# The last product of a gated merge block, eight token tiles in pairs by Strassen's scheme

## The reference, cut to what matters

```python
yb = ob @ w_o_dsa[l]                       # [1024, 1024] @ [1024, 1024]
ga, gb = jnp.split(jax.nn.sigmoid(gl), 2, axis=-1)
out = (ga * ya + gb * yb) @ w_out[l]       # the last product
x = x + gate[:, None] * out
return rms_norm(x, final_g)
```

## Time and profile before

| what | us |
|---|---|
| median of 3 runs (1383.16 to 1385.47) | 1385.27 |
| the profiled execution's own time | 1384.56 |
| its span, first to last instruction | 1382.8 |
| granted TensorE clock, mean over the span | 0.995 |
| busy: PE, DVE, ACT, POOL | 1340.8, 934.3, 705.9, 590.5 |

### The profile page before, as it was taken

The page is one execution under the profiler, slowest core; times in us unless marked ns, Lnnn a source line. Parts: engine busy times, 40 slices in busy tenths (PEclk is TensorE's granted clock), DMA queues, the critical chain, the costliest instruction groups (busy, mean ns, idle before and its releaser), DMA issues.

```text
span 1382.8 us, 26267 instructions
## 1 busy us (share of the span) xinstructions
PE 1340.8 (97%) x10010; PEld 808.4 (58%) x10010; DVE 934.3 (68%) x1894; ACT 705.9 (51%) x1461; POOL 590.5 (43%) x653
## 2 busy tenths in 40 slices
PE   6899999999999999999999999999999999899997
PEld 6456994444444556666666666655445777644444
DVE  4889877777334577678778776545834999737444
ACT  4767777785432654565665654333123777501111
POOL 0084677778762433632623521003021788665000
PEclk9999999999999999999999999999999999999999
DMA  9401333333324231322322322335675888975222
GB/s 367 149 8 32 109 111 105 115 123 107 115 87 131 70 88 49 92 64 64 92 64 63 93 64 77 107 107 211 201 237 184 148 157 161 153 270 178 74 92 92
DMA packets 213416, 166.36 MB, mean 120 GB/s; under 512 B 92482, under 2 KB 185514, under 8 KB 211628
## 3 DMA queue, kind: packets, MB, share of 16 engines
q1 hardware_dynamic: 212444, 160.20, 40.7%
q10 hardware_dynamic: 720, 4.46, 0.8%
q0 software_dynamic: 128, 0.03, 0.0%
HBM read 114.40 MB, written 31.15 MB: 105 GB/s over the span
## 4 chain that ended last, share of the span: by engine, by line
PE 50%; DVE 7%; issue 4%; POOL 3%; DMA 2%; ACT 1%; SPq 0%; DVEq 0%; ACTq 0%; POOLq 0%
PE ps L94 13%; PE ps L95 13%; PE ps L96 13%; DVE g_yq L1655 1%; DVE g_o L2581 1%; POOL g_shared L1420 1%; POOL g_shared L1422 1%; PE ps L1938 1%; PE ps L2062 1%; PE ps L2046 1%; PE ps L2045 1%; PE ps L2041 1%; PE ps L2061 1%; PE ps L1976 1%; DVE g_piece_hi L2592 1%
## 5 line engine op out<-in xcount | busy, mean ns | idle before, releaser
L94 PE MATMUL ps<-g_h_hi,g_piece_hi 128*128 128x512 f16 x544 | 206.9, 380 | 1.6 <-PEq L2689 1.6
L96 PE MATMUL ps<-g_h_hi,g_piece_lo 128*128 128x512 f16 x544 | 206.5, 380 | 0.0
L95 PE MATMUL ps<-g_h_lo,g_piece_hi 128*128 128x512 f16 x544 | 206.5, 380 | 0.0
L1420 POOL TENSOR_TENSOR g_shared<-g_shared 128x120 f32<-128x120 f32 (+14 forms) x120 | 56.3, 469 | 180.3 <-DMA g_shared<-diagonal_blocks 170.0
L1042 DVE TENSOR_SCALAR_CACHE_REDUCE a_ada<-a_ada,a_s_all 128x896 bf16<-128x896 f32 (+1 forms) x124 | 112.9, 967 | 1.0
L94 PE MATMUL ps<-g_o,g_h_hi 128*128 128x128 f16 (+2 forms) x424 | 102.0, 269 | 10.2 <-DMA g_o<-g_piece 7.6
L1655 DVE SCALAR_TENSOR_TENSOR g_yq<-e_raw,g_taps,g_yq 128x1024 f32<-128x1024 f32 x60 | 91.1, 1518 | 22.5 <-ACT g_yq L1484 20.7
L95 PE MATMUL ps<-g_o,g_h_hi 128*128 128x128 f16 (+2 forms) x424 | 101.8, 269 | 0.0
L96 PE MATMUL ps<-g_o,g_h_lo 128*128 128x128 f16 (+2 forms) x424 | 101.8, 269 | 0.0
L96 PEld LDWEIGHTS ps<-g_h_hi,g_piece_lo 128*128 128x128 bf16 x544 | 53.2, 98 | 64.3
L94 PEld LDWEIGHTS ps<-g_h_hi,g_piece_hi 128*128 128x128 f16 x544 | 53.2, 98 | 53.4 <-issue 2.0
(11 more groups left out here) (438 smaller groups left out, 4000.6 us busy)
## 6 DMA issues: line engine op xcount, KB each, us to landing
a_w<-in_w_in SPq DMA_DIRECT2D x17, 1024.0 KB, 5.8
g_piece<-in_w_in SPq DMA_DIRECT2D x34, 512.0 KB, 4.2
channel_gates<-a_ada SPq DMA_DIRECT2D x48, 256.0 KB, 2.2
g_shared<-diagonal_blocks SPq DMA_DIRECT2D x32, 256.0 KB
a_ada<-in_w_ada ACTq DMA_DIRECT2D x4, 1024.0 KB, 9.6
a_x<-in_x SPq DMA_DIRECT2D x8, 512.0 KB, 9.0
delta_gate<-a_ada SPq DMA_DIRECT2D x16, 256.0 KB, 2.6
g_shared<-sums_by_head SPq DMA_DIRECT2D x8, 512.0 KB, 4.1
```

The lines of the kernel that those rows point to most:

```text
L94: pe.matmul(out, a_hi, b_hi, start=first, stop=False)
L95: pe.matmul(out, a_hi, b_lo, start=False, stop=False)
L96: return pe.matmul(out, a_lo, b_hi, start=False, stop=last)
L1420: nc.gpsimd.tensor_tensor(part, table[:, j, :, j + 1:BASE], tc[:, :, j:j + 1].broadcast_to([P, NT, left]), ALU.mult).then_inc(sub, 1)
```

## The change

The last product is done for pairs of token tiles, tile i with tile i+4, in four groups. A group is a 2x2 block product: rows are the two tiles, the inner dimension is two halves of 512, and columns are two halves of 512. It is done in seven block products of 12 matmuls each, which add up in three PSUM banks: x takes products 0, 2, 4 and 6, y takes 1, z takes 3 and 5. Between them ScalarE copies a bank's state out (`keep`), since some results are partial sums. Each quarter of `w_out` (128 + 128 of its columns) now yields seven 128x512 operands, not four, and so does each group of tokens: three plain blocks and four sums or differences. GpSimd forms these four, all in place but the tokens' first. The merged half is no longer cast as it comes; it is kept in float32 (`m32`), scaled by SHRINK.

Who does what: ScalarE casts all seven `hi`; GpSimd makes the `lo` of the three plain blocks and the four sums; VectorE makes the `lo` of the four sums. `o` items stay as they were on GpSimd. SP loads a `w_out` item, and an `o` item, in two DMAs of 128 columns.

```diff
@@ SP @@
+                for half in range(2):
+                    c0 = u * UNIT + half * P if which == "o" else u * P + half * BANK
+                    sp.dma_start(w32[:, j % 2, :, half * P:(half + 1) * P], (wo if which == "o" else wv)[:, :, c0:c0 + P]).then_inc(w_in[j % 2], 16)
...
             for n in range(16):
+                sp.dma_start(m32[b // 4][:, b % 4, cols], g.m_dram[b * P:(b + 1) * P, cols]).then_inc(m_in[n % 4], 16)
                 if n >= 4:
                     sp.wait_ge(summed, n - 3)
+                sp.dma_start(gb[:, n % 4], g.sig_dram[2 * D + b * P:2 * D + (b + 1) * P, cols]).then_inc(gb_in[n % 4], 16)
-                if n in (1, 3, 5, 7):
-                    j = 2 + n // 2
-                    sp.wait_ge(split_ok, j - 1)
+                if n in (3, 5, 7, 9):
+                    j = 2 + (n - 3) // 2
+                    if order[j - 2][0] == "v":
+                        sp.wait_ge(v_turn, V_TURN + 4 * (order[j - 2][1] + 1))
+                    else:
+                        sp.wait_ge(split_ok, order[j - 2][1] - 1)
                     load(j)
@@ GpSimd @@
+            def final_weights(j, u):
+                low(B11)
+                low(B21)
+                low(B22)
+                nc.gpsimd.tensor_tensor(b22, b22, b12, ALU.subtract).then_inc(v_sum, 1)
+                nc.gpsimd.tensor_tensor(b12, b12, b11, ALU.subtract).then_inc(v_sum, 1)
+                nc.gpsimd.tensor_tensor(b11, b22, b11, ALU.add).then_inc(v_sum, 1)
+                nc.gpsimd.tensor_tensor(b21, b21, b11, ALU.subtract).then_inc(v_sum, 1)
...
+            def tokens(i):
+                token_low(i, A11)
+                token_low(i, A12)
+                pool.wait_ge(summed, 16)
...
+                nc.gpsimd.tensor_tensor(pair_sum[i % 2], a21, a22, ALU.add).then_inc(a_sum, 1)
+                nc.gpsimd.tensor_tensor(a11, pair_sum[i % 2], a11, ALU.subtract).then_inc(a_sum, 1)
+                nc.gpsimd.tensor_tensor(a21, a22, a11, ALU.subtract).then_inc(a_sum, 1)
+                nc.gpsimd.tensor_tensor(a12, a12, a11, ALU.subtract).then_inc(a_sum, 1)
+            def lower_right(i):
+                pool.wait_ge(kept, KEPT + 4 * i + 4)
+                nc.gpsimd.tensor_tensor(held[:, i % 2, 3], held[:, i % 2, 2], held[:, i % 2, 3], ALU.add).then_inc(both, 1)
+                nc.gpsimd.tensor_tensor(held[:, i % 2, 3], held[:, i % 2, 3], gate[:, UPPER], ALU.mult).then_inc(both, 1)
...
+            tokens(0)
+            token_low(0, A22)
+            for i in range(GROUPS):
+                if i + 1 < GROUPS:
+                    tokens(i + 1)
+                lower_right(i)
+                if i + 1 < GROUPS:
+                    token_low(i + 1, A22)
@@ TensorE, group i, product p @@
+                    if p in (A11, A12, A22):
+                        pe.wait_ge(a_low, A_LOW + 3 * i + (A11, A12, A22).index(p) + 1)
+                    else:
+                        pe.wait_ge(a_turn, A_TURN + 4 * i + p - 1)
+                    if p in (2, 4, 5, 6):
+                        pe.wait_ge(kept, KEPT + 4 * i + {2: 1, 4: 2, 5: 3, 6: 4}[p])
@@ ScalarE, group i @@
+                if i:
+                    rooted(0, 2 * i - 1)
+                    square(i - 1, 1)
+                    keep(i, 0)
+                    rooted(1, 2 * i)
+                if more:
+                    cast(i + 1, A11)
+                    cast(i + 1, A12)
+                keep(i, 1)
+                if more:
+                    cast(i + 1, S2)
+                keep(i, 2)
...
@@ VectorE @@
+                if n in (2, 4, 8, 12):
+                    final_weights((2, 4, 8, 12).index(n))
...
+                joined(i, 0, 1, 2, 0, LOWER)
+                if i == 0:
+                    token_lows(0, (S3, S4))
+                if not final:
+                    token_lows(i + 1, (S2, S1, S3, S4))
+                lower_right(i)
+                if final:
+                    dve.wait_ge(sq_ok, 2 * i + 1)
+                    nc.vector.tensor_tensor(x_of[1][:, 1, UPPER], x_of[1][:, 1, UPPER], fg[:, UPPER], ALU.mult).then_inc(mean, 1)
...
+                joined(i, 1, 2, 6, 0, UPPER)
+                lower_left(i)
+                averaged(0, 2 * i + (2 if final else 1))
+                lower_left_added(i)
+                finished(i, 0)
+                if not final:
+                    averaged(1, 2 * i + 2)
+                    finished(i, 1)
```

More of the change, by code:

```diff
@@ new lines, in _ @@
+            sp.wait_ge(proj, 16)
+            load_x(1)
+            for i in range(GROUPS):
+                for a in range(2):
+                    sp.wait_ge(done, 2 * i + a + 1)
+                    cols = LOWER if i == GROUPS - 1 and a else slice(0, D)
+                    sp.dma_start(g.out[0, (i + 4 * a) * P:(i + 4 * a + 1) * P, cols], y[:, a, cols]).then_inc(y_out[a], 16)
+                if i + 2 < GROUPS:
+                    load_x(i + 2)
+            sp.wait_ge(y_out[0], 16 * GROUPS)
@@ L2226, in _ @@
+            sp.wait_ge(y_out[1], 16 * GROUPS + 16)
         @block.gpsimd
@@ L2279, in _ @@
-            act.wait_ge(y_out[1], 16 * (NT // 2 - 1))
-            for part, (c0, c1) in enumerate(PARTS):
-                act.wait_ge(res, NT + part)
-                nc.scalar.activation(y[:, 1, c0:c1], x[:, 1, c0:c1], ACT.Square, accum_out=tail[:, part:part + 1]).then_inc(sq_ok, 1)
-            act.wait_ge(mean, NT + 3)
+            for j, (which, u) in enumerate(order):
+                if which == "v":
+                    act.wait_ge(w_in[j % 2], 16 + 32 * (j // 2 + 1))
+                    for p in CAST_V:
+                        if p in (T3, T1, T2, T4):
+                            act.wait_ge(v_sum, V_SUM + 4 * u + (T3, T1, T2, T4).index(p) + 1)
+                        nc.scalar.copy(v_hi[p][:, :, u * P:(u + 1) * P], v_source(j, p)).then_inc(v_cast, 1)
@@ new lines, in rooted, with last_square @@
+            def rooted(a, count):
+                act.wait_ge(mean, count)
+                nc.scalar.activation(ss[:, 2 * a + 1:2 * a + 2], ss[:, 2 * a + 1:2 * a + 2], ACT.Sqrt).then_inc(root, 1)
+            def last_square(part, cols, ready):
+                act.wait_ge(res, ready)
+                act.wait_ge(y_out[1], 16 * (GROUPS - 1))
+                nc.scalar.activation(y[:, 1, cols], x_of[1][:, 1, cols], ACT.Square, accum_out=tail[:, part:part + 1]).then_inc(sq_ok, 1)
+            for p in (A11, A12, S2):
+                cast(0, p)
@@ new lines, in _ @@
+            keep(0, 0)
+            for p in (S1, S3, S4, A22):
+                cast(0, p)
+            for i in range(GROUPS):
+                more = i + 1 < GROUPS
+                if i:
+                    rooted(0, 2 * i - 1)
[9 more added lines that the diff above has]
+                keep(i, 2)
+                if more:
+                    cast(i + 1, S1)
+                    cast(i + 1, S3)
+                keep(i, 3)
+                if more:
+                    cast(i + 1, S4)
+                    cast(i + 1, A22)
+                else:
+                    last_square(0, UPPER, 4 * i + 2)
+                square(i, 0)
@@ new lines, in lower_left_added, with averaged, finished @@
+            def lower_left_added(i):
+                dve.wait_ge(gate_ok, 5 * i + 5)
+                nc.vector.tensor_tensor(x_of[i % 2][:, 1, LOWER], x_of[i % 2][:, 1, LOWER], held[:, i % 2, 0], ALU.add).then_inc(res, 1)
+            def averaged(a, count):
+                dve.wait_ge(sq_ok, count)
+                nc.vector.tensor_scalar(ss[:, 2 * a + 1:2 * a + 2], ss[:, 2 * a:2 * a + 1], 1.0 / D, EPS, ALU.mult, ALU.add).then_inc(mean, 1)
+            def finished(i, a):
+                dve.wait_ge(root, 2 * i + a + 1)
+                nc.vector.reciprocal(ss[:, 2 * a:2 * a + 1], ss[:, 2 * a + 1:2 * a + 2]).then_inc(inv, 1)
+                dve.wait_ge(inv, 2 * i + a + 1)
+                nc.vector.scalar_tensor_tensor(out=y[:, a], in0=x_of[i % 2][:, a], scalar=ss[:, 2 * a:2 * a + 1], in1=fg,
+                                               op0=ALU.mult, op1=ALU.mult).then_inc(done, 1)
@@ L2346, in _ @@
+            dve.wait_ge(sq_ok, 2 * GROUPS + 1)
+            dve.wait_ge(mean, 2 * GROUPS)
+            nc.vector.scalar_tensor_tensor(out=tail[:, 3:4], in0=tail[:, 1:2], scalar=1.0 / D, in1=tail[:, 0:1],
+                                           op0=ALU.mult, op1=ALU.add).then_inc(mean, 1)
+            dve.wait_ge(root, 2 * GROUPS)
             nc.vector.reciprocal(tail[:, 0:1], tail[:, 3:4]).then_inc(inv, 1)
-            dve.wait_ge(inv, NT)
-            nc.vector.scalar_tensor_tensor(out=y[:, 1, BANK:D], in0=x[:, 1, BANK:D], scalar=tail[:, 0:1], in1=fg[:, BANK:D],
+            dve.wait_ge(inv, 2 * GROUPS)
@@ L2349, in _ @@
+            nc.vector.scalar_tensor_tensor(out=y[:, 1, LOWER], in0=x_of[1][:, 1, LOWER], scalar=tail[:, 0:1], in1=fg[:, LOWER],
                                            op0=ALU.mult, op1=ALU.mult).then_inc(done, 1)
```

282 lines of the change are left out of this document (161 added, 121 removed).

## The result

The changed kernel takes 1407.91 us (median of 6 runs, 1405.69 to 1412.64), the kernel before, run beside it, 1385.37 (6 runs, 1383.16 to 1388.24): ratio 1.0167, 95% interval 1.0152 to 1.0183. The prediction was 1412, with a range of 1392 to 1418.

A forecast was written before the change was run, and what follows sets the result against it. It took TensorE, without a gap in the merge, to bound the kernel before. Its terms, -10.4 + 6.2 + 5.9 + 1.0 + 5.9 + 12.4 + 5.6 = +26.6, plus 1 for the clock, took 1384.56 to 1412.2 us; range 1392 to 1418.

The forecast's parts named there:

- Fewer matmuls: Last product: 384 matmuls become 336, 48 fewer at 0.216 us each, -10.4 us.
- Block 8: Projection ahead of the last product: unit 2 of the weights loads late behind VectorE's `lo`, so TensorE stands, +6.2 us.
- split loads: Loads in two DMAs with 512-byte runs: counted as nothing; far end 2.6 us later per load, +5 us.
- Block 12: Projection ahead of the last product: unit 3 is loaded and split late, so TensorE waits, +5.9 us.
- Into the last product: Start of the last product: item 5 lands late, so ScalarE's cast of A11 and its `lo` are late, +1.0 us.
- Group 0: First group of the last product: sums, `lo` and `keep(0, 2)` come late, 0.3 + 1.9 + 1.0 + 2.7 = +5.9 us.
- The ring: Groups 1 to 3: the ordered chain over ScalarE, GpSimd and VectorE takes 22.3 us per group against TensorE's 18.1, +12.4 us.
- exclusion: Merge: a VectorE instruction with two SBUF operands and a GpSimd instruction never run side by side; each waits for the other.
- The tail: After the last matmul: a chain from `keep(3, 3)` to VectorE's last instruction takes 8.4 us, not 2.84, +5.6 us.
- The clock: TensorE after new gaps: first matmuls at 1.2 GHz lose 1.7 us per long gap; +1 us counted, far end 10.
- Dearer still: Rival: same steps, but the clock and split loads near their far ends, 1416 to 1421 us; chance 0.10.
- TensorE stays the bound: Rival: loads come early enough, only matmuls and tail count, -10.4 + 5.6 = -4.8, 1380 us; chance 0.06.

The follow-up runs named there:

- e7: The changed kernel with the edits of e4, e5 and e6, plus group 0's token sums and the lower-right sum and product moved to VectorE: 1379.4 us, ratio 0.9958.
- e8: The kernel before, with each unit of the last weights loaded by two DMAs of 128 columns instead of one of 256: 1384.9 us in its one run.
- e3: The changed kernel with VectorE's four `lo` of each output weight moved ahead of blocks 0, 3, 8 and 11: 9.8 us less by the ratios.
- e4: The changed kernel with units ordered v0, o2, v1, o3, v2, v3 and VectorE's weight `lo` ahead of blocks 0, 5, 9, 12: 13.9 us sooner.
- e2: The changed kernel with nearly all large two-SBUF-operand VectorE instructions of the last product reading one operand from PSUM (values wrong): 8.2 us less by the ratios.
- e5: The changed kernel with ScalarE's last-product queue reordered, early keeps and next casts ahead of the previous group's squares: 8.2 us sooner, 6.9 by the ratios.
- e6: The changed kernel, in the last group VectorE sums the second tile's upper half before multiplying its residual by the final gain: tail 5.75 us, ratio 1.0177.

## Why the prediction was right, and where it was not

Each step of it with what its profile shows:

1. *Fewer matmuls*, -10.4: right. e7 has 678 matmul records in 147.05 busy us; the kernel before 156.91, 9.9 more.
2. *Block 8*, +6.2: 8.1. The mechanism held link by link (gates, three blocks, four `lo`, load, GpSimd's pair). The gates landed at m+15.9, not 15.2; VectorE took 12.3 us for its part, not 11.5; the load took 6.15, not 5.8. The split loads, which I priced at nothing, took 1.5 (e8); I had only 0.7, for `m1`, which took 0.5.
3. *Block 12*, +5.9: 3.85. Unit 3 was ready at m+66.5, predicted 65.3. It was due later, as block 8 had started 1.8 later and its first matmuls ran at half clock, 1.4. Together the two waits are 12.0, predicted 12.1.
4. *Into the last product*, +1.0: no gap over 0.4 us there.
5. *Group 0*, 0.3 + 1.9 + 1.0 + 2.7: measured 0 + 1.85 + 0.93 + 2.66.
6. *The ring*, +12.4: 8.2. This is the term that I mis-sized most. Product 2 of the groups 1, 2 and 3 starts 21.6 and 21.4 us apart, not 22.3, and group 1's waits for `keep` are 1.55 and 0.77, together 2.3, not 5.1. Of the 2.8 missing there, 1.7 are matmuls that ran at half clock while TensorE would have waited: e3 and e4 show it, where the same wait is 1.56 with the fallen clock and 3.23 without. That exclusion and order make this wait, both of them, is shown by e2 and e5. One link I had not counted at all: ahead of the first root ScalarE loads a table for 1.28 us (at 1332.76). From the first square to the end of `keep(1, 0)` it takes 4.18 us, to that of `keep(2, 0)` 3.60, so it costs 0.6, once.
7. *The tail*, 8.4: 7.27. The order of the chain is right (e6). From `keep(3, 3)` to VectorE's end it takes 12.25 us, where I had 13.6.
8. *The clock*, +1: 5.2. Half of my reason holds: behind group 0, where the ring is the bound, the loss of 1.7 is given back by a shorter wait. But the matmuls after blocks 8 and 12 begin are the bound, and lose 1.4 and 1.7. I counted on six gaps of 2.88 us or more; there were two, and of three gaps of 2.65 to 2.67 one brought the clock down.

The sum was +27.6, the merge came out at +24.8: 5.8 too much in gaps and 1.3 in the tail's growth (+5.6, measured +4.3), 4.2 too little for the clock. The mechanism was right step by step, but that 1412 lies within 4 us of 1408 is partly luck: the terms that were too dear and the clock, which was too cheap, nearly cancel. The profiled execution reached the merge 3.2 us earlier than the one before, which no step could know; the medians are 22.5 apart. "Dearer still" was wrong in its split loads (1.5 us for what lands behind the first two and 0.35 for the third, not 2.6 for each) and half right in its clock. "TensorE stays the bound" was given 1380 at 0.06: for this kernel it is wrong. With other queues it comes true: e7, at 1379.4. The condition I named for it, unit 2 ready by m+32.5, is met there at m+23.1, by the order of the items and of VectorE's `lo`.
